# Decays spread by a DMA and a query-key product made transposed, in a two-layer mixer kernel

## The reference

```
cum[t]  = sum of g[s] for s <= t, within the block     (per b)
E[i, j] = exp(cum[i] - cum[j]) for j <= i, else 0
A       = beta_i * (k_i . k_j) * E[i, j]
QK      = (q_i . k_j) * E[i, j]
o       = ... + QK @ v_new
```

## Time and profile before

| | |
|---|---|
| median of the runs | 1899.18 us |
| the profiled execution's own time | 1898.54 us |
| its span, first to last instruction | 1896.7 us |
| busy: PE, DVE, ACT, POOL | 1888.9, 1459.9, 1083.9, 82.5 us |
| granted TensorE clock | 1.000 |
| DMA | 330.87 MB, 174 GB/s, queue of SP busy 53.8% |

### The profile page before, as it was taken

How to read it: one execution, slowest core, us unless ns; L and a number is a source line. 1 busy time by engine, 2 the same in 40 slices (tenths; PEclk the granted TensorE clock), 3 DMA queues, 4 the chain that set the end, 5 groups by cost and what they waited for, 6 DMA issues and landing times.

```text
span 1896.7 us, 32369 instructions
## 1 busy us (share of the span) xinstructions
PE 1888.9 (100%) x11791; PEld 1649.9 (87%) x11791; DVE 1459.9 (77%) x2316; ACT 1083.9 (57%) x1681; POOL 82.5 (4%) x61
## 2 busy tenths in 40 slices
PE   9999999999999999999999999999999999999999
PEld 9888998788988888889987888889888889888888
DVE  7777896877777777778777777777578888888887
ACT  6555764664555555467647645555346555675654
POOL 0000011010000000000110010000000000110000
PEclk9999999999999999999999999999999999999999
DMA  6666563445455555555534455555755665544654
GB/s 237 196 191 197 171 188 102 134 148 172 157 188 188 189 180 196 189 178 189 154 113 146 145 167 179 192 188 189 207 179 169 196 196 170 167 145 158 199 187 143
DMA packets 116717, 330.87 MB, mean 174 GB/s; under 512 B 10896, under 2 KB 40208, under 8 KB 116496
## 3 DMA queue, kind: packets, MB, share of 16 engines
q1 hardware_dynamic: 114496, 325.64, 53.8%
q10 hardware_dynamic: 2128, 3.94, 0.6%
HBM read 327.91 MB, written 1.64 MB: 174 GB/s over the span
## 4 chain that ended last, share of the span: by engine, by line
PE 94%; DVE 3%; ACT 2%; DMA 1%; issue 0%; POOL 0%; ACTq 0%
PE ps L2316 90%; DVE w_lo L1318 1%; PE ps L2342 1%; DMA raw<-stream 1%; ACT w_hi L615 1%; PE ps L2615 1%; PE ps L2865 0%; DVE sc L1830 0%; DVE arena L2131 0%; PE ps L3029 0%; PE ps L2806 0%; PE ps L2887 0%; PE ps L3001 0%; ACT gates L1112 0%; PE ps L2686 0%
## 5 line engine op out<-in xcount | busy, mean ns | idle before, releaser
L1318 DVE TENSOR_TENSOR w_lo<-raw,w_hi 128x1024 fp32r<-128x1024 f32 x614 | 750.2, 1228 | 220.6 <-ACT w_hi L615 219.2
L2316 PE MATMUL ps<-w_hi,a_both 128*128 128x512 f32 (+2 forms) x2368 | 753.2, 387 | 1.2 <-DVE a_both L2103 0.9
L615 ACT ACTIVATE w_hi<-raw 128x1024 fp32r<-128x1024 f32 x614 | 637.6, 1053 | 153.4 <-DMA raw<-stream 98.3
L2316 PE MATMUL ps<-a_both,w_hi 128*128 128x256 f32 (+1 forms) x3360 | 712.6, 342 | 0.0
L2316 PEld LDWEIGHTS ps<-a_both,w_hi 128*128 128x128 f32 x3360 | 580.7, 190 | 72.9 <-issue 0.8
L2316 PEld LDWEIGHTS ps<-w_hi,a_both 128*128 128x128 f32 x2368 | 441.9, 188 | 88.8 <-DVE a_both L2103 1.3
L2316 PE MATMUL ps<-w_lo,a_both 128*128 128x512 f32 (+2 forms) x1184 | 455.4, 385 | 0.0
L2316 PE MATMUL ps<-a_both,w_lo 128*128 128x256 f32 x2592 | 448.1, 283 | 0.0
L2316 PEld LDWEIGHTS ps<-a_both,w_lo 128*128 128x128 f32 x2592 | 380.5, 191 | 8.9
L2316 PEld LDWEIGHTS ps<-w_lo,a_both 128*128 128x128 f32 x1184 | 223.2, 188 | 36.5
L688 ACT ACTIVATE a_both<-arena 128x256 fp32r<-128x256 f32 x132 | 55.2, 418 | 139.1 <-DVE arena L1432 98.3
(11 more groups left out here) (348 smaller groups left out, 1185.1 us busy)
## 6 DMA issues: line engine op xcount, KB each, us to landing
raw<-stream SPq DMA_DIRECT2D x613, 512.0 KB, 3.6
arena<-upad SPq DMA_DIRECT2D x8, 284.0 KB, 6.4
gates<-late ACTq DMA_DIRECT2D x1, 1088.0 KB, 7.1
out<-tmp SPq DMA_DIRECT2D x3, 256.0 KB, 2.3
upad<-arena ACTq DMA_DIRECT2D x2, 288.0 KB, 7.4
con<-consts SPq DMA_DIRECT2D x1, 560.0 KB, 5.2
raw<-stream ACTq DMA_DIRECT2D x1, 512.0 KB, 3.7
x<-x_in ACTq DMA_DIRECT2D x2, 256.0 KB, 5.2
```

What stands on the lines that cost most here:

```text
L615: nc.scalar.activation(laid(w_hi, u), loaded(u), ACT.Copy).then_inc(hi_ready, 1)
L1318: V.tensor_tensor(laid(w_lo, u), loaded(u), laid(w_hi, u), ALU.subtract).then_inc(split_ready, 1)
L2316: return nc.tensor.matmul(o, a, b, start=start, stop=stop, **k)
```

## The change

What it does, in each of the two layers:

- PE no longer makes R. Instead DVE's copy of the cumulated sums is stored by SP in DRAM (`cumd`, 128 rows of 8 values, 4 KB) and read back by a second DMA so that each of the 128 partitions gets all 1024 values (512 KB, `rows`, in token-major order: a head's values lie 8 elements apart). SP issues the store right after `load` of moba+1, once `cumcp` is set, and the spread right after `load` of moba+4, once the store has landed.
- Et is computed by DVE from `rows`; PE's G no longer waits for `c_lo` (ktok does), and ktok no longer waits for Et.
- PE makes the product k.q instead of q.k, so QK comes out transposed; the transposes QKT and their copy by ACT are gone. For the decay factor a second array ET is made: DVE adds `rows` and a transposed mask after `moba_split(6, 7)`, ahead of kgd; ACT takes eight exponentials with the bias -cum (a new 128x8 array that DVE makes at `cumcp`), after its split of z unit 0 + 5 and ahead of the copy of T0; DVE multiplies the product by ET where it multiplied it by E.
- ET lies where sB is written later, so ACT's second square waits for DVE's QK.
- PE's wait for QK moves from ahead of `forward(1)` to the level `BASE` (its `T` products).

```diff
@@ constants @@
+    put("causalt", np.where(causal.T, 0.0, NEG).astype(np.float32))
@@ sync @@
+            def store_cum(l):
+                sp.wait_ge(*DV.at(l, "cumcp"))
+                sp.dma_start(cumd[l], sc[:, 72:80]).then_inc(cum_stored, 16)
+            def spread_cum(l):
+                sp.wait_ge(cum_stored, 16 * (l + 1))
+                sp.dma_start(flat(rows), cumd[l].rearrange("p b -> (p b)").unsqueeze(0).broadcast_to([PART, 8 * PART])
+                             ).then_inc(cum_spread, 16)
...
+                    for l in range(DEPTH):
+                        if u == POS["moba", l] + 1:
+                            store_cum(l)
+                        if u == POS["moba", l] + 4:
+                            spread_cum(l)
@@ scalar @@
                 split(POS["z", l] + AHEAD)
+                act.wait_ge(*DV.at(l, "ET"))
+                for b in range(8):
+                    e = nc.scalar.activation(ET[:, b, :], ET[:, b, :], ACT.Exp, bias=sc[:, 280 + b:281 + b])
+                e.then_inc(*AC.sig(l, "ET"))
                 turned_copy(0)
-                act.wait_ge(*PE.at(l, "QKT"))
-                nc.scalar.activation(QKT, ps[:, 4:6, :], ACT.Copy).then_inc(*AC.sig(l, "QKT"))
...
                         nc.scalar.activation(sA, flat(mqkv[:, 0:2, :]), ACT.Square)
+                        act.wait_ge(*DV.at(l, "QK"))
                         nc.scalar.activation(sB, flat(mqkv[:, 2:4, :]), ACT.Square).then_inc(*AC.sig(l, "mobasq"))
@@ vector @@
+                        tick(V.tensor_scalar(sc[:, 280:288], bank(6, 0, 8), -1.0, None, ALU.mult))
                         V.tensor_copy(sc[:, 72:84], bank(6, 0, 12)).then_inc(*DV.sig(l, "cumcp"))
...
-                dve.wait_ge(*PE.at(l, "R"))
+                dve.wait_ge(cum_spread, 16 * (l + 1))
                 for t in range(2):
-                    i = V.scalar_tensor_tensor(E[:, 4 * t:4 * t + 4, :], bank(6 + t).rearrange("p (a b) -> p a b", b=128), -1.0,
+                    i = V.scalar_tensor_tensor(E[:, 4 * t:4 * t + 4, :], rows[:, :, 4 * t:4 * t + 4].rearrange("p s b -> p b s"), -1.0,
                                                each(const("causal"), 4), ALU.mult, ALU.add)
...
                 moba_split(6, 7)
+                for t in range(2):
+                    i = V.tensor_tensor(ET[:, 4 * t:4 * t + 4, :], rows[:, :, 4 * t:4 * t + 4].rearrange("p s b -> p b s"),
+                                        each(const("causalt"), 4), ALU.add)
+                    if t == 0:
+                        tick(i)
+                i.then_inc(*DV.sig(l, "ET"))
                 dve.wait_ge(*PE.at(l, "ktok"))
...
+                dve.wait_ge(*AC.at(l, "ET"))
                 dve.wait_ge(*PE.at(l, "QK"))
                 for t in range(2):
-                    i = V.tensor_tensor(QK[:, 4 * t:4 * t + 4, :], bank(4 + t).rearrange("p (a b) -> p a b", b=128),
-                                        E[:, 4 * t:4 * t + 4, :], ALU.mult)
+                    i = V.tensor_tensor(QKT[:, 4 * t:4 * t + 4, :], bank(4 + t).rearrange("p (a b) -> p a b", b=128),
+                                        ET[:, 4 * t:4 * t + 4, :], ALU.mult)
@@ tensor @@
-                ev(DV, "c_lo")
-                for b in range(8):
-                    i = mm(bank(6 + b // 4, 128 * (b % 4), 128 * (b % 4) + 128), sc[:, 240 + b:241 + b].broadcast_to([PART, 128]), const("tri"))
-                i.then_inc(*PE.sig(l, "R"))
                 ev(AC, "gsq")
...
-                ev(DV, "Et")
+                ev(DV, "c_lo")
                 blocks(6, lambda o, tt, h: nc.tensor.transpose(o, kT(tt, h), ident), "ktok")
                 pe.wait_ge(m_ready, 3 * l + 3)
-                blocks(4, lambda o, tt, h: mm(o, qT(tt, h), kT(tt, h)), "QK")
+                blocks(4, lambda o, tt, h: mm(o, kT(tt, h), qT(tt, h)), "QK")
                 ev(DV, "kgd")
                 z_unit(0)
                 z_unit(1)
                 pair_turn(0)
-                ev(DV, "QK")
-                blocks(4, lambda o, tt, h: nc.tensor.transpose(o, QK[:, 4 * tt + h, :], ident), "QKT")
...
-                ev(AC, "QKT")
+                ev(DV, "QK")
```

More of the change, by code:

```diff
@@ L198 @@
     [("ident", 128), ("tri", 128), ("id64", 64), ("m0", 64), ("m0t", 64), ("mt", (LEVELS - 2) * 64), ("causal", 128),
-     ("cosm", TT * 32), ("sinm", TT * 32), ("cosl", TT * 16), ("sinl", TT * 16), ("rows", TAP_ROWS)])
+     ("cosm", TT * 32), ("sinm", TT * 32), ("cosl", TT * 16), ("sinl", TT * 16), ("rows", TAP_ROWS), ("causalt", 128)])
 LATE, N_LATE = columns([("dneg", 9 * 128), ("wa", 512), ("wx", 512)])
@@ L267 @@
 BASE = LEVELS - 2
-LV_STEPS = ([("T", 0), "QKT"] + [s for m in range(1, BASE) for s in (("U", m), ("X", m), ("T", m))]
+LV_STEPS = ([("T", 0)] + [s for m in range(1, BASE) for s in (("U", m), ("X", m), ("T", m))]
             + [("U", BASE), ("X", BASE), ("T", BASE), ("U", BASE + 1), ("T", BASE + 1)])
-PE_STEPS = (["cums", "cT", "R", "G", "stat", "AT", "vtok", "ktok", "QK"] + LV_STEPS
+PE_STEPS = (["cums", "cT", "G", "stat", "AT", "vtok", "ktok", "QK"] + LV_STEPS
             + ["u", "wT", "S1", "ob0", "wS", "oa", "mobakT", "ob1", "mobaT", "oT", "qT0", "qT1", "kT0", "kT1"])
-DVE_STEPS = (["z0", "cvar", "g", "cumcp", "gld", "silu", "c_lo", "Et", "gvar", "A", "X0", "kgd", "vb", "XT0", "QK", ("X", 1), ("X", 2), "mobavar"]
+DVE_STEPS = (["z0", "cvar", "g", "cumcp", "gld", "silu", "c_lo", "Et", "gvar", "A", "X0", "ET", "kgd", "vb", "XT0", "QK", ("X", 1), ("X", 2), "mobavar"]
              + [("X", m) for m in range(3, BASE)] + [("V", BASE), ("T", BASE + 1), "mobaqk"]
@@ L275 @@
                 "mlavark", "qrope", "mlak", "mlavarq"])
-ACT_STEPS = (["sm", "spe", "csq", "cn", "egc", "kds", "c_hi", "gsq", "E", "AT", ("T", 0), "QKT", ("U", 1), "mobasq"]
+ACT_STEPS = (["sm", "spe", "csq", "cn", "egc", "kds", "c_hi", "gsq", "E", "AT", "ET", ("T", 0), ("U", 1), "mobasq"]
              + [s for m in range(2, BASE) for s in (("T", m - 1), ("U", m))]
@@ L354, in build @@
         ev_scaled = sem("ev_scaled")
+        cum_stored, cum_spread = sem("cum_stored"), sem("cum_spread")
         cf_th, sc_copy, pair_read, b_read = sem("cf_th"), sem("sc_copy"), sem("pair_read"), sem("b_read")
@@ L455, in build @@
         QKT = E
+        ET = gup[:, 2048:3072].rearrange("p (a b) -> p a b", b=128)
         A = gup[:, 1024:2048].rearrange("p (a b) -> p a b", b=128)
@@ L513, in build @@
         wcomp = gr(4592, 4 * TAP_STEP * TAP_GROUPS)
+        rows = reg(11264, PART, 8)
+        cumd = [nc.dram_tensor(f"cumd{l}", (PART, 8), F32, kind="Internal").ap() for l in range(DEPTH)]
         upad = nc.dram_tensor("upad", (4 * PART, UPAD), F32, kind="Internal").ap()
```

## The result

The changed kernel takes 1906.33 us (median of 6 runs, 1905.55 to 1907.85) against 1899.11 us for the kernel before on the same chip: the ratio is 1.004 (95% interval 1.003 to 1.005). It is 7.2 us slower. The forecast was 1899.1 us, no change, with a range that ended at 1903.5. The profiled execution took 1906.36 us with a span of 1904.6 us, 7.9 us longer than before's span.

The account below looks back on a forecast made before the run. TensorE was taken as the bound, busy 1888.9 of 1896.7 us. Layer 0's +0.14 and layer 1's -0.27 gave -0.1, so 1898.4 profiled; the median, 0.64 above, made 1899.1 us, range 1895.7 to 1903.5.

Parts of the forecast that it names:

- the price of ET: On DVE ahead of kgd, the two ET instructions cost 0.9 us each, 1.8 a layer, 1.2 to 2.3.
- the sum for layer 1: At layer 1's kgd, DVE ready at 934.55 against 933.85: +0.70, less 0.97 for QKT, makes -0.27 us.
- the first gate: After QK, PE waits for DVE's kgd before z_unit(0); DVE was only 0.2 us ahead there.
- S: Delay of DVE's c_lo because the spread holds up moba+5's load: 0.97 us in layer 0, 0.64 in layer 1.
- absorbs nothing of S: DVE's 1.29 us gap at 268.97 moves as a whole with the late load, so c_lo's delay passes on in full.
- rival 2: The spread takes over 2.2 us, delaying kgd in both layers: 1904.7 us at 5, 1910.7 at 8; 20 in 100.
- rival 3: The 32-byte step makes each Et and ET instruction 1.15 us, ET 0.5 a layer dearer: 1900.1 us; 25 in 100.
- the upper bound: If every element at the 32-byte step took two turns, a DVE 128x512 instruction would cost some 1.15 us.
- Its surplus: Et's extra DVE time from the 32-byte step, 2 x 0.3 us, at most 1.08, falls free into the 1.29 gap.
- Rival 4: The spread does not hold up moba+5's load: -1.75 us, 1897.4, or 1896.2 with short instructions; 20 in 100.
- the slower side: Whole kernel slower by over 0.2% (3.8 us), from a slow spread and other slips: 20 in 100.
- Rival 1: Nothing gates PE at kgd, so the full 5.5 us is gained: 1893.7 us; 5 in 100 for over 0.2% faster.

Follow-up runs that it names:

- the packed pair: The changed kernel with the sums stored pair by pair in 4-byte packets, so Et and ET read consecutive elements: 1919.96 us.
- PE kept busy: The changed kernel with dummy TensorE transposes, 20 in layer 0 and 48 in layer 1, ahead of the wait for kgd: 1904.36 us.

## Why the prediction was wrong, step by step

**In short.** The first step that failed is the price of ET, 1.8 us, which the runs put at 2.96. Behind it two more failed: the sum for layer 1, which took nothing over from layer 0 and held a load's landing fixed, and the price of PE's wait, which had no term for the clock.

**What was right.** PE was the bound, R's 1.78 us left it (G starts where R did), QKT's gave 0.89 and 0.87 us instead of 0.97, and the first gate was kgd, in both layers. R's 3.6 us went into that wait. The exponentials on ACT were hidden, and PE never waited for the transposed product. In layer 0 the forecast had kgd ready at 284.54; it was ready at 283.86 + 0.67 = 284.53. That is luck: ET was forecast to start at 280.41 + 0.07 + 0.97 = 281.45 and started at 280.30, and it held kgd for 2.96 us instead of 1.8, two errors of 1.2 us in opposite directions.

**The queue of loads, S.** Priced at 0.97 and 0.64 us, it was 0 in both layers: c_lo never waited. The spread was priced at 2.2 us of queue; moba+5's load landed only 0.7 us slower in layer 0 (5.35 against 4.67 us) and 0.95 in layer 1 (5.37 against 4.42), and ACT's c_hi was done before DVE asked for it. The step that the gap behind Et "absorbs nothing of S" was wrong as well: the load that ends the gap did not move, so the gap took in all that came before it, and the split behind it started at 268.94 against 268.97. The spread landed after 4.9 us; rival 2, the slow spread, did not happen.

**ET, the step that failed first.** "For ET the whole 2 x 0.9 = 1.8 us counts, 1.2 to 2.3": it took 3.04 and 3.03 us, 2.96 to the next start, outside its own bounds. The 32-byte step makes it 1.03 us an instruction, shown by the packed pair at 1.28 against 2.15; that alone was within the bounds, halfway between the 0.9 assumed and rival 3's 1.15. The rest is GpSimd, whose mask products start when ET does and read SBUF as it does; taking them away gave 2.06 us. I had read nothing of GpSimd at this place, and none of the rows that made the upper bound had it beside them. Of the two pages of the Trainium skill that were weighed, one result a cycle ("VectorE: DVE Perf Modes", Mode 1x) does not hold for this step, and the cacheline note of "SBUF — State Buffer" has the right sign: the runs put the step at 1.7 times the packed price. The section that mattered was that page's other one, on who interferes with whom.

**Et.** Its surplus was to vanish in the gap behind it. In layer 0 it did (the gap went from 1.29 to 0.17 us). In layer 1 the gap stayed at 1.08 us, since the load behind it came late as well, and Et's 0.97 us counted.

**The sum for layer 1.** Forecast: -0.27 us, from layer 1's own slack, as if DVE entered it as before. Measured at kgd's first instruction: 939.62 against 932.35, 7.27 us late. The terms, each from a pair of rows: the load near 880 us was issued 2.16 us later (882.00 against 879.84), of which 1.59 is layer 0's loss passed on and 0.57 is not traced to a cause; it landed 1.70 us slower; the negation 0.07; Et 0.97; the two splits beside GpSimd 1.08; ET 2.96 to the next start; and the old gap of 1.60 closed. 2.16 + 1.70 + 0.07 + 0.97 + 1.08 + 2.96 - 1.60 = 7.34, 0.07 more than measured. The step that failed here is the one that let each layer be summed alone and took a load's landing to be fixed. The load was late with an instruction packet in its flight, and none of the rows read before the forecast says where that packet would fall.

**The clock.** The sum counted a wait as its length. The z units behind the two waits took 1.33 and 2.39 us more, at a granted clock of 0.79 and 0.67; with PE kept busy they ran at 1.00. This is 3.7 of the 7.9 us, and no term stood for it. Had kgd alone been 1.15 us late in layer 0, as forecast (1.11), the layer would have ended 0.26 us behind; it ended 1.59 behind, 292.26 against 290.67.

**The whole.** Layer 0: 1.15 (kgd) + 1.33 (clock) - 0.89 (QKT) = +1.59. Up to layer 1's forward(1): 940.94 - 933.85 = 7.09 for kgd, + 2.39 - 0.87 = +8.61 (949.70 against 941.09). Later 0.7 us comes back: before, PE had waited 1.3 us at L3001, and the change's list of waits has no such row. That leaves 7.9 us.

**The rivals.** None described it. Rival 4 had S = 0, which came true, and missed by 9 us with its 1897.4, for it took over ET's price, summed layer 1 alone and had no clock. The nearest in time was the slower side, given 20 in 100 for a slow spread, which is not what made it slow. Rival 1, the full gain, was called impossible because DVE ended too late. That holds for the order as written, but the order was a choice: with ET and the masks behind kgd, and the load undisturbed, the part is worth 5.1 of its 5.5 us (3.2 to 7.0 by the interval of the ratio).

## What to carry to other kernels

When work is taken off the bounding engine, put every new instruction of the engine that follows it behind what the bounding engine asks for next, and look at GpSimd's row for the same microseconds before pricing any DVE instruction with two SBUF operands. A wait of TensorE is priced with the clock behind it (here 8.6 us of waits cost 12.3), and where a ring of loads feeds the kernel, the lateness of one stage is followed through the loads into the next layer.

## What the runs showed of the hardware that was not expected

- A DVE instruction on 128x512 fp32 elements 32 bytes apart in SBUF starts its successor after 1.03 us, against 0.61 us for consecutive elements or for a PSUM bank.
- GpSimd products that read SBUF stretch DVE instructions with two SBUF operands from 2.06 to 3.04 and up to 4.1 us a pair, the weight splits from 2.35 to 3.45, and are stretched themselves from 2.56 to 4.42. The one that starts first grows less: ET by 1.0 to 1.1 us a pair where it was first, by 2.0 to 2.2 where GpSimd was. Instructions with one operand in PSUM keep their 0.67 us.
- With one 16 KB packet of an instruction queue in the flight of the 512 KB load near 880 us, that load landed after 4.85 to 5.5 us, without it after 3.3 to 3.5 (thirteen traces). Over all loads that had no other under way, a packet 0.5 to 2.5 us behind the issue went with over 3.7 us in 67 cases of 67, later ones in 8 of 108, none near in 19 of 1227. The packet's place moves with the number of instructions ahead of it: 72 more (36 matmul passes and their weight loads) brought it from 879.2 to 876.4 us. Why the load waits for it was not tried.
- A store of 4 KB in 4-byte packets took 11.1 us to land, in 32-byte packets 2.3 us. The three loads of 512 KB issued behind the former took 10.8 to 13.9 us in each layer, behind the latter 3.3 to 5.8.
- Behind waits of 1.99 and 2.18 us the z units ran at a granted clock of 1.00, behind waits of 2.29, 2.67, 3.16, 4.11 and 5.92 us at a mean of 0.77, 0.79, 0.77, 0.64 and 0.67, part of each stretch at the lower level. These are single traces: the ten runs of the kernels with 2.18 and 2.29 us differ in their granted clock (1.000 in some, 0.999 or less in others), so a wait of that length may or may not cost clock. With dummy transposes in the wait of the changed kernel it stayed at 1.00 in both layers.
